# Two-layer streaming trunk: layer one grouped as two tiles, then two and the streams' tile; the streams' states through three slots, two a step

## The reference

```
h  = rmsnorm(x) * (1 + scale1) + shift1
z, xbc, dt, lx, ly, g_ssd, g_lru = split(h @ w_in)
y, new_ssd = chunked Mamba-2 scan(silu(conv(xbc)), dt, state)     # 16 heads x 64, state 64
y_ssd = rmsnorm(y * silu(z))
y_lru = RG-LRU(conv(lx)) * gelu(ly)
x = x + g1 * (sig(g_ssd)*(y_ssd @ w_br_ssd) + sig(g_lru)*(y_lru @ w_br_lru)) @ w_out
h = rmsnorm(x) * (1 + scale2) + shift2
s1, s2 = q @ k1, q @ k2 ; top 16 of each, top 16 of the 256 sums -> 8 heads x 16 experts
x = x + g2 * sum_k gelu(h . u[e_k]) * g_k * v[e_k]                # 128 experts per token
```

## Time and profile before

| what | value |
|---|---|
| runs of the kernel before | 4569.81, 4576.07, 4576.73 us; median 4576.07 |
| profiled execution | 4574.72 us, span 4573.0 us |
| PE busy | 3224.7 us (71%) |
| DVE busy | 2828.0 us (62%) |
| ACT busy | 1474.3 us (32%) |
| POOL busy | 1445.4 us (32%) |
| DMA packets | 1610.83 MB, mean 352 GB/s |
| gather queue (q0) | 1342.26 MB, 72.0% of 16 engines' span |

### The profile page before, as it was taken

How to read it: one execution, slowest core, us unless ns; L and a number is a source line. 1 busy time by engine, 2 the same in 40 slices (tenths; PEclk the granted TensorE clock), 3 DMA queues, 4 the chain that set the end, 5 groups by cost and what they waited for, 6 DMA issues and landing times. The chain is left out here.

```text
span 4573.0 us, 60410 instructions
## 1 busy us (share of the span) xinstructions
PE 3224.7 (71%) x21986; PEld 1901.7 (42%) x21986; DVE 2828.0 (62%) x6591; ACT 1474.3 (32%) x4662; POOL 1445.4 (32%) x1298
## 2 busy tenths in 40 slices
PE   7899994677777664589999855766777665444443
PEld 4455552445455442345455523444555443121111
DVE  2422058796854578478834696955854578675554
ACT  2224012443622222253722323433622223232222
POOL 0000002443333334333333324433433434444332
PEclk9999996878888886599999976878888886555555
DMA  8343327999999999889999979999999999999997
GB/s 329 133 152 102 101 79 313 394 375 408 417 418 419 411 416 381 364 340 342 362 366 401 380 275 363 390 377 395 418 418 419 414 415 367 421 420 421 421 421 332
DMA packets 279860, 1610.83 MB, mean 352 GB/s; under 512 B 56410, under 2 KB 61328, under 8 KB 112524
## 3 DMA queue, kind: packets, MB, share of 16 engines
q0 software_dynamic: 184320, 1342.26, 72.0%
q1 hardware_dynamic: 75280, 256.81, 15.0%
q10 hardware_dynamic: 19964, 7.91, 0.6%
HBM read 1597.63 MB, written 7.91 MB: 351 GB/s over the span
## 5 line engine op out<-in xcount | busy, mean ns | idle before, releaser
L571 POOL DMA_INDIRECT ring<-in_peer_uv,units x1280 | 1442.2, 1127 | 3092.7 <-PE psum L976 2157.5
L1863 DVE SCALAR_TENSOR_TENSOR ring<-ring,hrow 128x1024 f32<-128x1024 f32 x1280 | 1539.5, 1223 | 883.6 <-DMA ring<-in_peer_uv,units 857.8
L976 PE MATMUL psum<-ring,diag 128*32 128x256 f32 x10240 | 925.5, 493 | 1150.5 <-ACT diag L1341 1148.3
L584 PE MATMUL psum<-hT,wslot 128*128 128x384 f32 (+1 forms) x4224 | 1277.4, 459 | 8.9 <-ACT region L1234 3.1
L584 PEld LDWEIGHTS psum<-hT,wslot 128*128 128x128 f32 x4224 | 840.2, 203 | 442.8 <-issue 102.8
L976 PEld LDWEIGHTS psum<-ring,diag 128*32 128x32 f32 x10240 | 320.9, 130 | 1665.7 <-ACT diag L1341 1344.2
L1331 ACT ACTIVATE gel<-hid 128x2 f32<-128x2 f32 x640 | 129.1, 202 | 1864.1 <-DVE ring L1863 1782.9
L584 PE MATMUL psum<-region,wslot 128*128 128x384 f32 (+1 forms) x1536 | 460.1, 456 | 3.4 <-ACT region L1234 1.9
L584 PEld LDWEIGHTS psum<-region,wslot 128*128 128x128 f32 x1536 | 303.2, 202 | 154.9 <-issue 30.7
L1341 ACT ACTIVATE diag<-pick,wgt 128x32 f32<-128x32 f32 x1280 | 331.6, 306 | 0.0
L1335 ACT ACTIVATE wgt<-gel,units 128x1 f32<-128x1 f32 x1280 | 307.3, 287 | 21.0
(11 more groups left out here) (247 smaller groups left out, 2800.2 us busy)
## 6 DMA issues: line engine op xcount, KB each, us to landing
wslot<-in_w_tiles SPq DMA_DIRECT2D x360, 512.0 KB
ring<-in_w_modt SPq DMA_DIRECT2D x24, 2048.0 KB, 8.8
ring<-in_peer_uv,units POOLq DMA_INDIRECT x1280
wslot<-in_w_gate SPq DMA_DIRECT2D x32, 128.0 KB
region<-in_states_t SPq DMA_DIRECT2D x16, 256.0 KB
region<-in_states_n SPq DMA_DIRECT2D x16, 256.0 KB
out_new_ssd_sample<-region ACTq DMA_DIRECT2D x16, 256.0 KB
xT<-in_x_t SPq DMA_DIRECT2D x1, 2560.0 KB, 9.1
```

The costliest lines, as they stand in the source:

```text
L571: pool.indirect_dma_start(ring[:, n, :], None, table, bass.IndirectOffsetOnAxis(ap=units[:, s % 2, block, 0, quad:quad + 1].bitcast(U32), ...
L584: last = pe.matmul(out, wslot[:, n % SLOTS, k * P:(k + 1) * P], src(k), start=k == 0, stop=k == KT - 1)
L976: last = pe.matmul(psum[c * BLOCK:(c + 1) * BLOCK, block % 2, block // 2 * 256:(block // 2 + 1) * 256], diag[:, n, :], ring[:, n, D + c * ...
L1863: dve.scalar_tensor_tensor(out=ring[:, n, 0:D], in0=ring[:, n, 0:D], scalar=1.0, in1=hrow[:, e % 2, :], op0=ALU.mult, op1=ALU.mult, accum_ ...
```

## The change

Layer one is grouped as tiles 0, 1 (256 columns) and tiles 2, 3 and the streams' tile (384 columns). Layer two keeps tiles 0, 1, 2 and tiles 3, 4. Region 1 now makes the experts of tile 2, whose gathering begins at pair 128, so its window is pairs 16 to 122. Regions 2 and 3 keep their windows.

A group of three tiles with the streams has less room, so the states' buffers are three single slots (each `states_t` piece uses two of them, 0 and 1; `states_n` goes round all three), `tail_rows` has three rows and not seven, and the state work takes two pieces a step. All 16 loads of a layer now stand together on SP, ahead of weight Z4, and ACT waits for the last stores ahead of the fill of LX.

```
-FIRST, COUNT = (0, 3), (3, 2)
+GROUPS = (((0, 2), (2, 3)), ((0, 3), (3, 2)))
+REGION = [(l, *group) for l in range(DEPTH) for group in GROUPS[l]]
...
-    b["Z"] = b["S"] + (19 if g == 0 else 15)
+    b["Z"] = b["S"] + 6 * COUNT[r] + (4 if r in ENDS else 1)
...
+SPANS = (None, (16, 122), (201, 314), (329, 500))
...
-    window(fresh + pairs_of(1, 2), steps_of(1), 0, 64 - 28 + 125)
...
+def state_slot(i):
+    return i % 2 if i < 8 else (i - 8) % 3
...
-                def states(l, loads):
+                def states(l):
+                    for i in range(16):
+                        slot = state_slot(i)
+                        if 2 <= i < 10:
+                            sp.wait_ge(S["yoff"], at("yoff", l, i - 2))
+                        elif i == 10:
+                            sp.wait_ge(S["dec"], l + 1)
+                        elif i > 10:
+                            sp.wait_ge(state_out[slot], 16 * state_stores(l, i - 11))
...
-                            if g and j == 4:
-                                states(l, range(13))
+                            if r == ENDS[l] and j == 4:
+                                states(l)
                             yield load(tile(l, TZ + j))
...
-                            if g and j < 3:
-                                states(l, (13 + j,))
...
-                        if 11 <= i <= 18:
-                            j = i - 11
-                            act.wait_ge(S["sadded"], at("sadded", l, j))
-                            act.dma_start(dst[:, l, j, :, :], lay.states[:, (8 + j) % 5, :]...)
+                        if 12 <= i <= 15:
+                            for j in (2 * i - 24, 2 * i - 23):
+                                act.wait_ge(S["sadded"], at("sadded", l, j))
+                                act.dma_start(dst[:, l, j, :, :], lay.states[j % 3]...)
...
                         if i == 1 and lay.sample:
-                            act.wait_ge(written, r // 2 * 256 + 32)
+                            act.wait_ge(written, lay.l * 256 + 32)
+                            for j in range(5, 8):
+                                act.wait_ge(state_out[j % 3], 16 * state_stores(lay.l, j))
```

More of the change, by code:

```diff
@@ L36 @@
 TILES_E = DEPTH * NT
-FIRST, COUNT = (0, 3), (3, 2)
-T0 = (0, 3 * P)
-NG = (3 * P, 2 * P)
-PN = (3 * P, P)
-REGIONS = 2 * DEPTH
+GROUPS = (((0, 2), (2, 3)), ((0, 3), (3, 2)))
+REGION = [(l, *group) for l in range(DEPTH) for group in GROUPS[l]]
+REGIONS = len(REGION)
+LAYER, FIRST, COUNT = zip(*REGION)
+OPENS = [LAYER.index(l) for l in range(DEPTH)]
+ENDS = [OPENS[l] + len(GROUPS[l]) - 1 for l in range(DEPTH)]
+STARTS = {LAYER[r] * NT + FIRST[r]: r for r in range(REGIONS)}
+KEPT = {s: i for l in range(DEPTH) for i, s in enumerate(s for s in range(l * NT, l * NT + NT) if s not in STARTS)}
+SLOTS_KEPT = max(KEPT.values()) + 1
 TZ, TX, TLX, TLY, TGS, TGL, TBS, TBL, TOUT, TWQ, TILES = 0, 8, 18, 26, 34, 42, 50, 58, 66, 74, 90
@@ L69, in bases @@
     return b
-BASE = [bases(r % 2) for r in range(REGIONS)]
+BASE = [bases(r) for r in range(REGIONS)]
 LENGTH = [BASE[r]["END"] for r in range(REGIONS)]
@@ L137, in steps_of @@
         return [(r, i) for i in range(LENGTH[r])]
-    window(fresh + pairs_of(1, 2), steps_of(1), 0, 64 - 28 + 125)
-    window(pairs_of(3, 4), steps_of(2), 9, 122)
-    window(pairs_of(5, 6, 7), steps_of(3), 9, 180)
+    queue = fresh + pairs_of(*range(1, 8))
+    begun = PAIRS - len(fresh)
+    for r in range(1, REGIONS):
+        until = (SPANS[r + 1][0] if r + 1 < REGIONS else 8 * PAIRS) - begun
+        window(queue[:until], steps_of(r), SPANS[r][0] - begun, SPANS[r][1] - begun)
+        queue, begun = queue[until:], begun + until
     window(pairs_of(8), [(REGIONS + t, i) for t in range(3) for i in range(FINAL)], 9, 60)
@@ L166 @@
 LOADS = 98
-TILE0 = [NT * (r // 2) + FIRST[r % 2] for r in range(REGIONS)]
+TILE0 = [NT * LAYER[r] + FIRST[r] for r in range(REGIONS)]
 def loads_in(r, i):
@@ L192, in same_group @@
 def same_group(s):
-    return s % NT not in (2, 4)
+    return s + 1 < TILES_E and s + 1 not in STARTS
 def within(s):
@@ L393, in __init__ @@
                 self.lacc = room(24 * N + 2 * (self.pad + 1), self.pad + 1)
-                self.lru = [room(18 * N + i * N, N) for i in range(9 if g else 8)]
+                self.lru = [room(18 * N + i * N, N) for i in range(8)]
                 self.qT = room(10 * N, 2, 2, N)
@@ L1005, in turn_h @@
                     pe.wait_ge(E["h_rows"], 2 + turned["h"])
-                    if t in FIRST and block == 0 and s and half == 0:
-                        r = 2 * l + FIRST.index(t)
+                    if s in STARTS and block == 0 and s and half == 0:
+                        r = STARTS[s]
                         pe.wait_ge(S["modulated"], at("modulated", 2 * r + 1, 7))
-                        if G[r % 2].sample:
+                        if G[r].sample:
                             pe.wait_ge(S["sampled"], at("sampled", l, 1))
@@ L1081, in fill @@
                         act.wait_ge(S["conved"], at("conved", r, j - 2))
+                    if not lay.first:
+                        act.activation(x[:, 0:HIST], carry[:, j, :], ACT.Copy)
                     if not lay.sample:
@@ L1395, in _ @@
                 act.wait_ge(written, WRITTEN + 16 * NT)
-                for slot in range(5):
-                    act.wait_ge(state_out[slot], 16 * sum(1 for l in range(DEPTH) for j in range(8) if (8 + j) % 5 == slot))
+                for slot in range(3):
+                    act.wait_ge(state_out[slot], 16 * state_stores(DEPTH - 1, 6 + slot if slot < 2 else 5))
             @block.vector
@@ L1497, in x_stage @@
                 def x_stage(r, i):
-                    l, g = divmod(r, 2)
-                    lay = G[g]
+                    lay = G[r]
+                    l = lay.l
                     n = lay.nt * HEADS
                     v = dt[:, 0:lay.nt, :].rearrange("p t h -> p (t h)")
-                    if i == 0 and not lay.sample:
+                    if i == 0 and lay.first:
                         dve.memset(lay.xpad[:, :, 0:HIST], 0.0).then_inc(S["zeroed"], 1)
@@ L1541, in ssd_tile @@
                             dve.wait_ge(S["silued"], at("silued", r, 9))
-                            if r == 2:
+                            if l and lay.first:
                                 dve.wait_ge(written, 256)
@@ L1637, in lx_stage @@
                 def lx_stage(r, i):
-                    lay = G[r % 2]
-                    if i == 0 and not lay.sample:
+                    lay = G[r]
+                    if i == 0 and lay.first:
                         dve.memset(lay.lpad[:, :, 0:HIST], 0.0).then_inc(S["zeroed"], 1)
```

305 lines of the change are left out of this document (152 added, 153 removed).

## The result

| | before | after |
|---|---|---|
| runs on one chip | 4565.33 to 4576.73 us, median 4569.81 | 4599.39 to 4620.29 us, median 4607.85 |
| profiled execution | 4574.72, span 4573.0 | 4607.85, span 4606.1 |

The ratio is 1.0076, with an interval from 1.0058 to 1.0095: the kernel is 0.8% slower, 35 us (the two medians stand 38 us apart). The forecast's 4636 us was 61 us above the profiled execution of before, on which it was built, and this one is 33 us above it. The time lies within the range.

What follows compares the result with a forecast made beforehand. Region 0's 713 us were taken as bound by PE, partly ACT and DVE, then 3860 us around the gather. -163 - 7 + 216 + 17 = +63 on 4574.7 us gave 4638, say 4636 us; range 4570 to 4695.

Steps and rivals of the forecast that it cites:

- The start: Region 0, up to the first unit: 256-column projections instead of 384 gain 1.7 us each, 163 us in all.
- Pairs 0 to 16: Beside the end of Q: one tile less of top-16 gives 7 us back, from 94 to 87.
- Region 1: Pairs 16 to 122 beside 384 columns: window 917 us; with the pairs behind it up to 201, +216 us.
- The exchange: Region 1: state stores and the loads waiting for them cost 45 us, ends 0 and 123.
- the price of one round trip: Region 1, store then load: 17 us for the first, 9 and 9 for the next two, as the gather runs dry.
- B: Region 1: the streams cost 46 us, the exchange nothing; 4576 us in all, chance 0.15.
- The streams' other work: Region 1: S 25 us, state pieces' work in Z 9, split fills, taps, tails and small work 12.
- load waits: S of region 1: state loads only two ahead, 8 us each, half hidden, in three steps: 12 us.
- Region 3: The same exchange beside a DMA-bound stretch: 28 us less some 11 of before, +17, ends 0 and 80.
- A: Exchange and streams' work both hidden: region 1 841 us, region 3 0; 4545 us in all, chance 0.11.
- C: No rush of packets: each round trip costs a full 41 + 8 us; 4810 us at most, 4720 likelier, chance 0.12.
- D: Region 0: the start gains only 135 us; 4664 us in all, its chance counted within the forecast's 0.62.

Runs made afterwards that it cites:

- e2: Kernel after without seven of each layer's eight stores of the streams' state, loads waiting for the piece's last use: 4569.48 us, 0.9985 of before.
- e4: Kernel after without the loads of pieces 2 to 7 of `states_t`, PE reading pieces 0 and 1 instead: 4588.71 us, 1.0038 of before.
- e5: Kernel before without seven of each layer's eight stores of the streams' state: 4545.48 us, 0.9941 of before.
- e1: Kernel after with layer one grouped as before and region 1 in pairs 16 to 177, three state slots kept: 4594.46 us, 1.0043 of before.
- e7: Kernel before with the odd stores of the streams' state issued by SP, not ACT: 4578.26 us, 1.001 of before.
- e9: Kernel before with the streams' eight state stores a layer issued by POOL on the gather's own queue: 4559.16 us, 0.997 of before.
- e6: Kernel after with stores 1, 3, 5, 7 and half of the prompt's issued by SP, not ACT: 4610.15 us, 1.0079 of before.

## Why the prediction was right, and where it was not

**The start.** -163 forecast, -166 measured. The sum held, and so did most of its terms. From the first projection of each stage, before and after: X with S gave 37 us (35 forecast), Z 15 and LX 14 (14 each), LRU 6.5 (6), M 52 (54). OUT with its norm gave 17 (14), and the norm ahead of X 6.5, where 2 were counted for all norms; Q gave only 19 (24), and these mostly cancel.

**Pairs 0 to 16.** -7 forecast, -3 measured. The row to trust was the pace of the DMA: 90.5 us with DMA at 0.99 leaves nothing more to take.

**Region 1.** 917 forecast, 906 measured. 7 of the 11 us are the model's, region 2, which was 840 before and reads 833 after. Inside the sum two terms were mis-sized and cancelled, so the closeness of the sum is luck. The exchange was put at 45 us, and its stores were worth 12.7 (e2). The step that failed is the price of one round trip: 50 packets a us and 10 to 12 us for the gather to run dry were taken from region 3, where the DMA is full. In region 1 it is not. The window in which store 0 was issued there (868.89), after:

```profile
865.00:870.00 5.00, 5.00 (x28) 2.40 (x27) 3.67 (x7) 1.49 (x6) 1.10 (x2) 1.00 0.19 45
```

PE is busy with the mixer, POOL waits 10.45 us for a slot until 868.6, and the gather has nothing under way till then: DMA share 0.19. From 868 to 871 1004 small packets pass beside 12 of the gather. The load goes out at 875.8 and is used at 880.45, with the gather running again, and the first wait is 7.3 us. So there was nothing left to run dry. Rival B had this as its condition, and it was half true: the stores got through sooner, though not for nothing. The streams' other work was put at 25 + 9 + 12 = 46 us, 12 of them load waits. This is the second step that failed. The load waits were 9 in S (e4). The rest was put at 34 and comes to about 66. It is worked out stage by stage against region 2 of the same profile, with 2.1 us for each pair by which the stages differ:

| stage | region 1 (pairs) | region 2 (pairs) | extra |
|---|---|---|---|
| N1, X | 105.2 (11) | 100.7 (12) | 7 |
| S | 114.4 (12) | 82.3 (11) | 30 |
| Z, LX | 136.3 (15) | 109.9 (16) | 28 |
| LRU | 72.8 (9) | 67.7 (10) | 7 |
| M | 206.1 (27) | 210.2 (30) | 2 |
| OUT, N2 | 82.8 (10) | 68.3 (10) | 14 |
| Q | 188.8 (22) | 193.8 (24) | -1 |

That is 88 in all before rounding, where the forecast had 91. Less the exchange's 13 and the 9 of load waits, some 66 are left. 14 of them are in OUT and N2, to which the forecast gave nothing. What makes the 66 up was not tested; it is a ledger of two regions of one profile.

**Region 3.** +17 forecast, +7 measured. The three waits came with 27.7 us, and most of that is absorbed by the gather's backlog, as the forecast argued. e5 against e2 gives 19 - 13 = 6 us for the stores' part.

**Pairs behind the window.** 64 pairs from 137 on at 5.03 us were forecast. 1616 to 1935 is 319 us for them, 4.98 a pair.

**Region 2.** Nothing was forecast; it reads -7. e1, e5, e7 and e9, which leave region 2 as it was before, show 900 to 904, so the 912.1 of before is a slow reading of one profile.

**The rivals.** A, the exchange hidden and the streams' work with it, is refuted by e2 (12.7 us and PE's idle time in it) and by the 88 us of both together, where it needed under 36. The prediction's estimate of 2.6 us for a store wasn't met either: even in region 1, with little of the gather under way, 7 us passed from store 0 to the load behind it. B, the streams cost and the exchange doesn't, is nearer on the exchange than the forecast (13 us against its 0 and the forecast's 45), but its 46 us for the streams were 75, and its 4576 was missed. C, no rush, is refuted by 39.3 us of waits in six, 6.5 each, where it wanted 49. D, a start of only 135, by the 166.

So the forecast's direction came from rows that held (80 projections against 106 pairs beside 384 columns). Its sum of +63 was 30 us above the ledger's +33: 14 in region 1 and the pairs behind it, 10 in region 3, 7 of scatter in region 2 and 3 at the start, less 4 in pairs 0 to 16.

## What to carry to other kernels

A wait that stops the consumer of a deep prefetch ring can last until the ring has run dry: so it was at the first wait of region 3, whether the small packets of a store or the load behind them came last, and fewer packets or a second queue did not shorten it much. It was not so in region 1, where the gather was idle when the store was issued. So look at what the ring is doing at that moment, and ask for slack in slots before asking for bandwidth. Work beside a window that the compute engines bound costs what those engines need for it (2 us a pair here), and outside it what the DMA needs (5 us), so fill such a window. The same edit paid in the kernel with five buffers and cost in the one with three, so try a change of queue together with the number of slots.

## What the runs showed of the hardware that was not expected

- A store of 1024 runs of 256 bytes costs POOL only 0.94 us to issue on the software queue, and becomes 80 packets there by the queue's count (1280 for 16), against 1040 on q10 ((19964 - 3324)/16, the first of them in the earlier trace rows).
- ACT is held while it issues a store when others are queued, 16.96 us before and 12.88 after; with 2 KB runs 1.68.
- From a store's issue to the use of what is loaded behind it, 19.5 to 22.2 us passed with 1024 to 2048 small packets ahead, beside a full gather; with the DMA at a share of 0.19 when the store was issued, 11.6 us (868.89 to 880.45).
- Queues that have packets take turns one for one, as the prediction had it, and a second small queue gets turns of its own: 664 packets of 256 bytes beside 666 of 8 KB in 12 us (after), and with two small queues 425 and 424 beside 424 in 8 us (e6). The gather kept 96.4% and 91.3% of the engines' time in these windows.
- TensorE's granted clock fell to 0.50, its lower level of 1.2 GHz, in the window from 3075, PE having stood since 3070, stayed there until 3088 though PE was busy again from 3084, and was 0.96 in the window from 3088.
